# The stationary activation parts of the expert values, moved 32 and 16 bytes off a multiple of 64

## What is computed

```python
    def chunk(args):
        hc, ec, gc = args
        u = peer_u[ec]
        a = jax.nn.gelu(jnp.einsum("ckd,cd->ck", u, hc).astype(jnp.float32)) * gc
        vv = peer_v[ec]
        return jnp.einsum("ck,ckd->cd", a.astype(vv.dtype), vv)
```

## The kernel before, in words

| tensor | address | over 128 |
|---|---|---|
| w_hi (two tiles), w_lo (two tiles) | 32896, 36992, 41088, 45184 | 0 |
| act_parts | 57472 | 0 |
| h_hi, h_lo | 57504, 65696 | 32 |
| mem_lo | 81248 | 96 |
| y, m, f and x parts | 96608 and on, in steps of 8192 and 24576 | 96 |

## Time and profile before

### The profile page before, as it was taken

One profiled execution on the slowest core, in us unless ns is written; L12 is line 12 of the kernel. 1 busy time (PEld: TensorE's weight loads), 2 busy tenths in 40 slices (PEclk: granted clock), 3 DMA queues, 4 the chain that ended last, 5 costly groups with the idle time before them and its releaser, 6 DMA issues.

```text
span 1618.8 us, 33492 instructions
## 1 busy us (share of the span) xinstructions
PE 1591.3 (98%) x12571; PEld 1496.6 (92%) x12571; DVE 1093.1 (68%) x1860; ACT 899.4 (56%) x1252; POOL 893.0 (55%) x413
## 2 busy tenths in 40 slices
PE   8999999999999999999999999999999999999997
PEld 7999899999999999988888888889998899999997
DVE  7998645779943777778888667675844496555522
ACT  6567766455565444444444445556676654666642
POOL 8786468868885000000000344467876589788885
PEclk9999999999999999999999999999999999999999
DMA  6565345656666555555555666664544365566663
GB/s 216 169 193 150 104 134 182 184 170 191 185 182 191 169 170 175 163 167 181 168 179 177 207 195 189 195 189 138 188 127 124 101 177 173 176 190 187 188 186 114
DMA packets 86216, 277.00 MB, mean 171 GB/s; under 512 B 11233, under 2 KB 18161, under 8 KB 86129
## 3 DMA queue, kind: packets, MB, share of 16 engines
q1 hardware_dynamic: 85856, 274.77, 55.2%
q0 software_dynamic: 272, 1.05, 0.2%
HBM read 274.73 MB, written 1.05 MB: 170 GB/s over the span
## 4 chain that ended last, share of the span: by engine, by line
PE 89%; DVE 4%; POOL 2%; issue 2%; ACT 2%; DMA 0%; DVEq 0%; SPq 0%; ACTq 0%; POOLq 0%
PE gemm L661 35%; PE gemm L939 21%; PE gemm L666 18%; PE aux L1186 4%; PE gemm L748 3%; PE aux L913 2%; POOL w_lo L455 1%; ACT w_hi L1272 1%; PE gemm L693 1%; PE gemm L682 0%; POOL w_lo L451 0%; PE aux L880 0%; PE gemm L734 0%; DVE big L2357 0%; PE gemm L699 0%
## 5 line engine op out<-in xcount | busy, mean ns | idle before, releaser
L455 POOL TENSOR_TENSOR w_lo<-raw,w_hi 128x1024 fp32r<-128x1024 f32 (+1 forms) x330 | 798.2, 2428 | 304.3 <-ACT w_hi L1272 291.8
L1272 ACT ACTIVATE w_hi<-raw 128x1024 fp32r<-128x1024 f32 (+1 forms) x492 | 515.1, 1049 | 564.6 <-PE gemm L661 303.8
L661 PE MATMUL gemm<-h_hi,w_hi 128*128 128x256 f32 x2096 | 293.6, 282 | 1.8 <-PE aux L880 0.7
L661 PE MATMUL gemm<-h_lo,w_hi 128*128 128x256 f32 x2144 | 294.5, 279 | 0.4 <-DVE mem_lo L1859 0.4
L666 PE MATMUL gemm<-h_hi,w_lo 128*128 128x256 f32 x2096 | 289.1, 280 | 2.7 <-POOL w_lo L455 2.0
L661 PEld LDWEIGHTS gemm<-h_lo,w_hi 128*128 128x128 f32 x2144 | 269.3, 188 | 1.0 <-DVE mem_lo L1859 0.9
L661 PEld LDWEIGHTS gemm<-h_hi,w_hi 128*128 128x128 f32 x2096 | 264.5, 188 | 5.0 <-issue 3.3
L666 PEld LDWEIGHTS gemm<-h_hi,w_lo 128*128 128x128 f32 x2096 | 263.2, 188 | 5.6 <-POOL w_lo L455 4.3
L455 DVE TENSOR_TENSOR w_lo<-raw,w_hi 128x1024 fp32r<-128x1024 f32 x162 | 196.4, 1221 | 106.3 <-ACT w_hi L1272 105.7
L939 PE MATMUL gemm<-w_hi,act_parts 128*128 128x512 f32 x1024 | 254.9, 391 | 0.0
L939 PEld LDWEIGHTS gemm<-w_hi,act_parts 128*128 128x128 f32 x1024 | 191.0, 188 | 39.1
(11 more groups left out here) (413 smaller groups left out, 2106.2 us busy)
## 6 DMA issues: line engine op xcount, KB each, us to landing
raw<-in_w_u SPq DMA_DIRECT2D x128, 512.0 KB, 3.6
raw<-in_w_ev SPq DMA_DIRECT2D x128, 512.0 KB, 3.6
raw<-in_w_up SPq DMA_DIRECT2D x48, 512.0 KB, 4.2
raw<-in_w_gate SPq DMA_DIRECT2D x24, 512.0 KB, 3.6
raw<-in_w_down SPq DMA_DIRECT2D x24, 512.0 KB, 3.5
raw<-in_w_conv_in SPq DMA_DIRECT2D x16, 512.0 KB, 4.1
raw<-in_w_peer_q SPq DMA_DIRECT2D x16, 512.0 KB, 3.6
raw<-in_w_branch SPq DMA_DIRECT2D x24, 288.0 KB, 2.9
```

Source lines behind the costliest of these rows:

```text
L455: eng.tensor_tensor(w_lo[v][:, 0:n], raw[c.raw][v][:, 0:n], w_hi[v][:, 0:n], ALU.subtract).then_inc(lo_ready[v], 1)
L661: mm = pe.matmul(out, w[:, k, :], act_part[:, k, :], start=(n == k == 0), stop=False)
L1272: act.activation(w_hi[v][:, 0:n], raw[c.raw][v][:, 0:n], ACT.Copy).then_inc(hi_ready[v], 1)
```

## The change

act_parts becomes one dimension of 2048 + 8 floats. The low parts come first and start 4 floats, 16 bytes, into it; the high parts take the second half and start 8 floats, 32 bytes, past its middle. Over a multiple of 128 bytes, a_lo then lies 16 and a_hi 32. The tensor's space is still given back at once, and 32 bytes longer it ends where h_lo begins (57472 + 8224 = 65696), so no other tensor moves. Instructions, their order, their waits and the loads stay the same.

```diff
--- before.py
+++ after.py
@@ -186,7 +186,7 @@
         w_hi = [sb(f"w_hi{v}", [P, TILE], F32R) for v in range(2)]
         w_lo = [sb(f"w_lo{v}", [P, TILE], F32R) for v in range(2)]
         xres = sb("xres", [P, KD, T])
-        with nc.sbuf_tensor("act_parts", [P, KD, T], F32R) as act_parts:
+        with nc.sbuf_tensor("act_parts", [P, KD * T + 8], F32R) as act_parts:
             pass
         sb("ahead_of_h", [P, 8])
         h_hi = sb("h_hi", [P, KD, T], F32R)
@@ -296,7 +296,9 @@
             "p b n (g i o) -> p b n g i o", g=GROUP // 2, o=2)
         hot2 = carve(2, GROUP // 2 * P * 2, dt=F16).rearrange("p b (g i o) -> p b g i o", g=GROUP // 2, o=2)
 
-        a_hi, a_lo = [act_parts[:, i:i + 4, :].rearrange("p (c v) t -> p c v t", c=2) for i in (0, 4)]
+        AHEAD_LO, AHEAD_HI = 4, 8
+        a_hi, a_lo = [act_parts[:, i:i + 4 * T].rearrange("p (c v t) -> p c v t", c=2, v=2)
+                      for i in (4 * T + AHEAD_HI, AHEAD_LO)]
         memT = small[:, 0:KD * T].rearrange("p (k t) -> p k t", t=T)
 
         carve = carver(big, KD * T)
```

## The result

The kernel with the moved parts takes 1630.57 us (median of 6 runs, 1629.86 to 1631.6), the kernel before 1621.07 in the 6 runs beside them. The ratio is 1.0056, with a 95% interval from 1.0046 to 1.0067. That is slower by 9.5 us, where 5.1 us of gain were forecast, and outside the range, which ended at 1624.

What follows compares the result with a forecast made beforehand. TensorE's matmul steps were taken to bound the expert-values stage. Saving 3.3 ns on each of 1536 steps, 5.1 us, from the profiled 1620.51 gave 1615.4, plus 0.43 for the median 1615.8 us; range 1604 to 1624.

Steps and rivals of the forecast that it cites:

- What bounds the kernel: Expert values (L939): the stage lasts TensorE's start-to-start step, 226.7 ns, times 1536 matmuls; no other engine holds it.
- (a): 256-column products: moving tile 32 bytes ahead of stationary, modulo 128, is quick; 96 ahead costs 1.6 ns more.
- (B): Rival, expert values: only part of the disturbance goes, 1.7 ns a step, 2.6 us saved, 1618.3 us; chance 0.14.
- The price, 24 of 32 clocks kept: Expert values: 24 clocks over the column count stay anywhere; 8 clocks, 3.3 ns, are place and go, saving 5.1 us.
- (C): Rival, expert values: place does nothing for time, 32 clocks are what 512 columns cost anywhere, 1620.9 us; chance 0.17.
- (A): Rival, expert values: the whole disturbance goes, step 217.5 ns, 1604.9 us or 1606.8; chance 0.16.
- (D): Rival, expert values: slower, loads meet moving reads; 1625.8 us if paid per column (0.13), 1623.4 per load (0.05).
- The writes, the seats, the tail: act_parts' new write places and exchanged halves cost nothing; at the stage's end 0.06 us of gain is lost, left out.
- What was said of proof: L939's ungated step would tell the cases apart, forecast 223.4 ns; 256-column products must keep 116.7 and 118.3.

Runs made afterwards that it cites:

- both_128: Kernel before the change with both parts 128 bytes past their old place and a spare 256 bytes ahead of h: 1629.53 us, ratio 1.0046.
- the probe: TensorE alone, rest of the kernel left out, stationary tile shifted in 16-byte steps up to 496: 226.7 ns at distance 0, 512 columns.
- swap_only: Kernel before the change with only the halves of act_parts exchanged, both parts still on a multiple of 128 bytes: 1621.07 us, ratio 0.9995.
- low_only: Kernel before the change with only the low parts 16 bytes past a multiple of 128, halves not exchanged: 1621.76 us, ratio 0.9999.
- all_64_behind: Kernel before the change with h, mem_lo, x, y, m and f moved to 64 bytes behind the weights: 1605.91 us, ratio 0.9919.

## Why the prediction was wrong, point by point

**What bounds the kernel: right.** The stage is TensorE's steps times 1536, before and after, with no other engine in the chain. The slowdown is in the step: 4.0 us in the gated half (15 pieces, 12.25 us from start to start against 11.98) and 4.9 in the ungated one (3.27 in the long piece, 1.62 in the last), which makes the 8.9 us read from the ends of the stage.

**(a), the address rule: wrong in its modulus.** The rows were read as 32 ahead, quick, and 96 ahead, slow, modulo 128. All of rows 7 to 10 hold as well modulo 256, where they read +32 and -32 (116.7 and 118.4 in the table). No row of before could tell the two apart, since w, h and mem_lo have no other pair of distances. both_128 does, and so does the probe, where shifts 0 and 256 have 226.7 and shift 128 has 233.4. By either reading the change moves the high parts to the slower side of the two, as (B) said; yet the forecast gave both parts a gain, from a price that it took from another width.

**The price, 24 of 32 clocks kept: wrong, and the step that failed.** The prediction took the 24 clocks over the column count of the quickest row with 256 columns as what every product of this type keeps. It put the other 8 of the 512-column step, 3.3 ns, down to place, and counted them as gained: 223.4 ns. The step became 233.1. The table shows that 24 wasn't the least with 256 columns: 113.3 ns is 16 clocks over. And the 32 clocks with 512 columns are the least of all places tried: 226.7 ns is 544 clocks, twice 272. The least overhead measured grows with the columns, 16 for 256 and 32 for 512, and no place that was tried had any gain to give. (C) had this, "32 clocks are what 512 columns cost anywhere", right as the least and wrong as the most.

**(A), down to 217.5: wrong.** Rows 12 are bf16 on one tile of zeros; no fp32 step came near it in any place. Nor did the 215.8 ns that the prediction has from the Trainium skill ("TensorE: Matmul & The Clock Gate", section "Back-to-back issue gap") show up: the least steady fp32r step with 512 columns is 226.7.

**(D), slower: the right sign, a mechanism that isn't shown, a price too small by half.** Its reason was a stationary tile "off its line". both_128 is slow with every tile on a multiple of 128 bytes, and -16 can be quick off one, so the line isn't what counts; that loads and moving reads meet is left as a possible reason, which no trace shows. For the price it took 1.6 ns as the difference of places and doubled it, 3.2 ns. Measured are 6.2 ns ungated, 5.4 gated, 6.7 between the steady 226.7 and 233.4. The places with 256 columns don't order those with 512: distance 0 is the best with 512 (226.7) and among the worst with 256 (120.0). "0 ahead may be the best distance, which nothing in the trace rules out" was the sentence to weigh more than its 0.13: with no row at 0 and 256 columns, neither the size of the price nor its sign could be taken over from them.

**Every place equal, in (C): contradicted.** The same 1536 matmuls and loads, with the same data and neighbours, step by 226.9 or 232.5 ns by their place alone (swap_only against both_128); the probes, where nothing else runs, differ likewise. The sentence of the Trainium skill cited there ("SBUF — State Buffer", section "SBUF: two separate sides") would, as the prediction read it, have given no difference; the measurement decides. What the ports do isn't seen in any trace; the probes show only that no other engine is needed for the difference.

**The writes, the seats, the tail: right.** Over the whole stage L1475 has 630 ns and L2195 1391, and the same lines of before 628 and 1393. In the ungated stretch of after they have 630 and 1939 ns, where rows 13 have 626 and 1945. swap_only and low_only, which write to new places too, take the time of before. The end has the same order as the earlier trace rows.

**What was said of proof: useful.** The forecast named 229.9 ns for (D) in the ungated stretch and as its danger a phase "that settles in another steady pattern". The first was exceeded. The second was seen: the low parts are free in one sequence and cost the stage's last 2 us in another. A third sign misled: "The 256-column products must keep 116.7 and 118.3", or else place isn't the cause. They had 117.8 in the expert scores, but so had swap_only, where the stage is as quick as before.

**Open.** Why the hardware has these distances and patterns isn't shown; the modulus (for 512 columns and whole shifts of 256), the table and the dependence on the entry are. Which entry leads to which pattern couldn't be foretold, and whether the distance and the entry are all that counts isn't settled, as +16 shows. The part of the gain that all_64_behind lost in longer steps isn't traced to its causes.

## What to carry to other kernels

When TensorE is the bound and each matmul has its own fp32r load, note for each kind of product the distance between moving and stationary start modulo 256 bytes. Measure its step at the kernel's own column count and in the kernel itself, since a probe's entry can differ: here 0 was best with 512 columns and 64 behind with 256, and each was poor at the other width. A price read at one width, or a rule of alignment fitted to two distances, isn't evidence for a third. Before moving a tile that all of a stage's time goes through, run a probe over the distances to see whether the present one is already the best; distance 0 was.

## What the runs showed of the hardware

- A matmul of fp32r with a new 128x128 stationary tile steps by 226.7 to 239.9 ns with 512 columns and by 113.3 to 121.5 with 256, by the distance of the two start addresses and by the entry; with 512 columns 4 bytes more or less already matter (226.7 at 0, 236.4 at +4, 232.4 at -4).
- The distance counts modulo 256 bytes (16 pairs of shifts with 512 columns). Equal shifts of both tiles by 32 or 64 change nothing under equal entries; between +16 made by w and +16 made by a the steps differ (231.7 and 226.7 to 228.3), and why isn't shown.
- A stream with unchanged places has more than one steady pattern (226.7 and 233.3 at -16 with 512 columns; 113.3 and 117.8 at +64 and at -64, 116.7 and 117.8 at +32, with 256). What ran before it bears on which one it is, and it can last for 34 tiles, 96 us. Products that no edit touched can so differ by 1 us between two profiled executions (before and swap_only).
